# Four weight buffers at 32, 64, 128 and 256 bytes past multiples of 2048: a float32 network in three-product form

## The reference

```
h = rms_norm(x, norm_mlp[i])                                  # (512, 1024)
x = x + jnp.square(jax.nn.relu(h @ w_mlp_up[i])) @ w_mlp_down[i]
x = x + (p[i] @ w_ple_proj[i]) * jax.nn.sigmoid(x @ w_ple_gate[i])
...
u = h @ w_in                                                  # third block
ff = jnp.square(jax.nn.relu(h2 @ w_ff1)) @ w_ff2
```

## Time and profile before

| | us |
|---|---|
| runs of the kernel | 3722.1, 3724.81, 3724.98 (median 3724.81) |
| the profiled execution, its own time | 3728.49 |
| its span, first to last instruction | 3726.7 |
| TensorE busy (PE) | 3385.8 (91%) |
| TensorE weight loads (PEld), beside PE | 2664.8 (72%) |
| VectorE busy | 2026.8 (54%) |
| ScalarE busy | 1304.6 (35%) |
| GpSimd busy | 393.0 (11%) |
| DMA, mean rate over the span | 74 GB/s |

### The profile page before, as it was taken

The page is one execution under the profiler, slowest core; times in us unless marked ns, Lnnn a source line. Parts: engine busy times, 40 slices in busy tenths (PEclk is TensorE's granted clock), DMA queues, the critical chain, the costliest instruction groups (busy, mean ns, idle before and its releaser), DMA issues.

```text
span 3726.7 us, 50818 instructions
## 1 busy us (share of the span) xinstructions
PE 3385.8 (91%) x20970; PEld 2664.8 (72%) x20970; DVE 2026.8 (54%) x3555; ACT 1304.6 (35%) x2143; POOL 393.0 (11%) x336
## 2 busy tenths in 40 slices
PE   6898899999899999998996889978999989999998
PEld 4667777777676677786765666566777767777886
DVE  5454446664423456654555435578787872455443
ACT  3233233222323332223333234455555532324221
POOL 0001200000000000000001000035444520000000
PEclk9898899999898999999997989999999998999999
DMA  3120024442352124432320120031111102232321
GB/s 126 60 68 1 1 80 133 135 139 76 69 96 60 35 96 136 136 113 80 113 66 19 47 85 12 29 97 40 39 39 42 55 5 85 69 117 91 102 92 67
DMA packets 318853, 274.90 MB, mean 74 GB/s; under 512 B 10913, under 2 KB 310049, under 8 KB 317857
## 3 DMA queue, kind: packets, MB, share of 16 engines
q1 hardware_dynamic: 314368, 256.07, 22.7%
q10 hardware_dynamic: 4256, 15.58, 1.1%
HBM read 265.34 MB, written 6.29 MB: 73 GB/s over the span
## 4 chain that ended last, share of the span: by engine, by line
PE 77%; DVE 13%; ACT 5%; issue 3%; DMA 1%; POOL 1%; DVEq 0%; ACTq 0%; SPq 0%; POOLq 0%
PE ps L95 75%; DVE f L107 4%; DVE f L101 3%; DVE r L101 3%; PE ps L98 2%; ACT f L88 2%; DVE f L104 1%; ACT r L92 1%; ACT L88 1%; POOL f L101 1%; ACT f L92 1%; DVE f L113 1%; DVE f L110 1%; ACT f L89 0%; DVE r L107 0%
## 5 line engine op out<-in xcount | busy, mean ns | idle before, releaser
L95 PE MATMUL ps<-r,r 128*128 128x512 f32 x10368 | 2463.7, 396 | 124.0 <-DVE r L101 88.1
L95 PEld LDWEIGHTS ps<-r,r 128*128 128x128 f32 x10368 | 1928.5, 190 | 604.1 <-issue 183.1
L95 PE MATMUL ps<-f,f 64*64 64x64 f32 (+10 forms) x9648 | 878.0, 274 | 169.4 <-issue 48.6
L95 PEld LDWEIGHTS ps<-f,f 64*64 64x64 f32 (+4 forms) x9648 | 654.1, 161 | 366.6 <-issue 181.1
L101 DVE TENSOR_TENSOR r<-f,r 128x1024 fp32r<-128x1024 f32 (+2 forms) x621 | 657.8, 1065 | 464.2 <-ACT r L92 457.3
L92 ACT ACTIVATE r<-f 128x1024 fp32r<-128x1024 f32 (+2 forms) x548 | 506.6, 937 | 782.9 <-PE ps L95 661.7
L92 ACT ACTIVATE f<-ps 128x512 f32<-128x512 f32 (+3 forms) x422 | 189.8, 465 | 639.9 <-PE ps L95 388.2
L101 POOL TENSOR_TENSOR f<-f,f 128x512 f32<-128x512 f32 (+2 forms) x280 | 350.9, 1267 | 489.0 <-ACT f L88 273.6
L107 DVE SCALAR_TENSOR_TENSOR f<-f,f,f 128x128 f32<-128x128 f32 (+3 forms) x622 | 365.2, 592 | 26.5 <-ACT f L88 7.3
L101 DVE TENSOR_TENSOR f<-ps,f 128x512 f32<-128x512 f32 (+4 forms) x325 | 178.0, 560 | 340.3 <-PE ps L95 330.2
L88 ACT ACTIVATE f<-ps 128x512 f32<-128x512 f32 (+3 forms) x203 | 112.0, 553 | 622.3 <-PE ps L95 620.2
(11 more groups left out here) (32 smaller groups left out, 741.3 us busy)
## 6 DMA issues: line engine op xcount, KB each, us to landing
f<-in_w_mlp_up SPq DMA_DIRECT2D x32, 1024.0 KB, 6.0
f<-in_w_mlp_down SPq DMA_DIRECT2D x32, 1024.0 KB, 6.2
f<-in_w_ff SPq DMA_DIRECT2D x32, 1024.0 KB, 5.1
f<-in_w_ada SPq DMA_DIRECT2D x48, 512.0 KB, 3.9
f<-in_w_in SPq DMA_DIRECT2D x24, 1024.0 KB, 4.9
f<-in_w_in SPq DMA_DIRECT2D x44, 512.0 KB, 3.5
f<-in_w_in_even SPq DMA_DIRECT2D x12, 1024.0 KB, 5.2
f<-in_w_in_odd SPq DMA_DIRECT2D x12, 1024.0 KB, 12.4
```

Of the source, the lines that this page charges most:

```text
L95: return self.e.matmul(out, l, r, start=first, stop=last)
```

## The change

The allocation of the two high and the two low weight buffers. Before each, `K.at` is moved on, so that the buffers start at these distances past a multiple of 2048 bytes: the high ones 8 and 16 words (32 and 64 bytes), the low ones 32 and 64 words (128 and 256 bytes).

```
-        self.whi = [K.take(1024)[1] for _ in range(2)]
-        self.wlo = [K.take(1024)[1] for _ in range(2)]
+        self.whi, self.wlo = [], []
+        for home, phase in ((self.whi, 8), (self.whi, 16), (self.wlo, 32), (self.wlo, 64)):
+            K.at += (phase - K.at - K.slab // 4) % LINE if phase < LINE else (phase - K.at - K.slab // 4) % 128
+            home.append(K.take(1024)[1])
```

## The result

The changed kernel takes 3758.99 us (median of 4 runs, 3752.86 to 3768.01) against 3724.89 us before: a ratio of 1.0092, 95% interval 1.0075 to 1.0108, or +28 to +40 us. The forecast was 3757 us.

A forecast was written before the change was run, and what follows sets the result against it. The prediction took TensorE's rate of one-pass products as the bound; 7,500 products at 4.3 ns gave +32 us, all other terms 0, so 3724.8 + 32 = 3757 us, 0.9% slower. The range was 3720 to 3815 us, holding 0.79.

The forecast's parts named there:

- What bounds the kernel: TensorE, busy 91% of the span: the time is the rate of its one-pass products, 226.7 ns from start to start.
- The price of a product: One-pass products with shifted stationary operands: 231.0 ns instead of 226.7, so 4.3 ns more for each.
- the piece with 8 columns: Existing weight piece whose tiles start 32 bytes apart; its products took 231.0 ns, from which the 4.3 ns price was read.
- The count: One-pass products that pay the price: 7,500 taken, at least 5,957, at most all 9,984; +32 us in all.
- The grid: Weight buffers leaving multiples of 512 bytes cost 4.3 ns a product; 256 bytes was given the same price as 128.
- Moving operands: Weights streamed from shifted buffers: 5 us at most, counted 0; some 2,000 products streaming later stages' activations already in the count.
- ScalarE and VectorE: The 416 copies and 416 subtractions at the new addresses: taken as 0.
- Plain float32: Products at 431 ns a record, 2.2 ns beyond the columns each pass; used to bound a possible gain at -104 us.
- TensorE's busy time: In the profile after the change, PE busy time up by some 30 us.
- no change: Rival, 3725 us: the 4 ns come from the narrow load or 32-byte steps, not the buffer's start; chance 0.26.
- Faster: Rival, 3622 to 3690 us: the 13.3 ns are a stream-load collision at equal addresses modulo 512, resolved by shifting; chance 0.19.
- Much slower: Rival, 3800 to 3825 us: each product loses a further 13.3 ns, a rate of 240 ns; chance 0.13.

The follow-up runs named there:

- high alone: Against the kernel before: high buffers at 32 and 64 bytes, low ones at 0, region behind the buffers at 256 bytes; 3766.75 us, ratio 1.0098.
- narrow_pitch: Against the kernel before: narrow weight pieces (8 and 24 columns) stored 256 bytes from one kt to the next, not 32 and 96; 3724.57 us, ratio 0.9997.

## Why the prediction was right, and where its steps were not

- **What bounds the kernel:** right. The loss of 35.3 us is in the one-pass products, and TensorE's unbroken pieces got longer in proportion (2.0% in the yardstick), with nothing else moved.
- **The price of a product:** forecast 231.0 ns, 4.3 more; measured 231.4 in the window above, 4.7 more. One of the two places that it was read from, the piece with 8 columns, did show the cause (the narrow pieces at 256 bytes apart). That the products behind a wait have the same 231 is not shown to be the same thing. That the size fits to 0.4 ns is in part luck: the piece is a mix of seven distances, the change another mix, and single distances cost from 2.2 to 6.7 ns.
- **The count:** right. Compared product by product in the two traces (those whose next product starts within 260 ns in both), 7,570 products that had 226 or 227 ns before have 231.6 on the mean after, and 1,550 others went from 231.7 to 232.1, as the prediction had it for those behind waits. The forecast took 7,500.
- **The grid:** wrong. I took a start off the multiples of 512 bytes for the cause, and gave 256 bytes the price of 128. The low buffer at 256 bytes is free, and so is all at 256. The total came out since the piece that uses it also uses a high buffer at 64 bytes, and a piece with some costly loads pays most of the price: high alone costs the whole loss. This is luck.
- **What is measured from where:** not seen. I looked at the address of the load alone. In this change x, h and hh stay at multiples of 2048 bytes and the region at one of 256, so the address of the load and its distance from the stream are the same number, and the forecast could be right with the wrong one. With x shifted and the weights in place the loss is +0.83%, with both shifted alike it is none that can be told.
- **Moving operands:** counted at 0, with "some 2,000" for those of the stages. They are 2,880 of the 9,984 (2,976 with those of 256 columns), and at 256 bytes they are free. The 432 products of 512 columns in which the weights stream were put at nothing too; with buffers at 32, 64 or 128 bytes they have a price like the others, some 2 us.
- **ScalarE and VectorE:** 0, as forecast.
- **Plain float32:** its 431 ns were misread. The products overlap at the change of kind; by length they are (7.03 - 0.59) / 15 = 429 ns apart, 0.59 us being the duration of one in the groups by form of that stretch, so 1.3 ns a pass lie beyond the columns and not 2.2. The bound of the faster rival moves by some 9 us, the forecast not at all.
- **TensorE's busy time:** forecast +30 us, measured +45.1, of which 9.6 are the clock of this execution.
- **The rivals:** no change fell with the result itself, and its reasons, the narrow load or the steps of 32 bytes, were settled by the narrow pieces: the width has no part, the addresses have. Faster, with a collision at equal addresses that a shift resolves, is the reverse of what was found: equal addresses are the best of the seven distances measured (0, 32, 64, 128, 192, 224, where x is ahead of the weights, and 256 bytes). Distances that are no multiple of 32 bytes were not tried. Much slower was priced at 240 ns; the worst steady rate measured is 233.4.

That a weight load takes nothing from the running matmul, as the Trainium skill says ("TensorE: Matmul & The Clock Gate", Step-by-step), does not hold here to the last 3%: the same loads and streams run at 226.7 or at 233.4 ns a product by their distance alone. The Trainium skill (same page, Back-to-back issue gap) gives N/2.4 + 2.5 ns, 215.8 for 512 columns, as the gap of an isolated matmul. No steady stretch of one-pass products of any kernel here, all with a load beside each, reached it.

## What to carry to other kernels

Where a weight load runs beside a stream of a one-pass float32r product, let both start at the same place modulo 256 bytes; it needs neither multiples of 2048 nor of 256, and padding one side alone is what costs. Look at the distance from start to start in an unbroken stretch, to 0.1 ns: in these kernels a steady 226.7 with a duration of 389 ns is the good state, a pattern that averages 229 to 233 with 391 to 396 ns is another, and a price of 2 to 3% of TensorE's time shows in no wait and on no other engine. When one address moves by padding, all that is taken behind it moves too, so read the whole list of what starts where.

## What was not expected of the hardware

- The price depends on the distance between two reads modulo 256 bytes and is not symmetric: 6.7 ns a product at 32 and 64 bytes, 5.7 at 128, 2.2 at 192 in the last stage but 6.7 in another stretch of the same kernel, and 6.7 again at 224 (x at 32 bytes, weights at 0). Since all streams beside one another start at the same place modulo 256, the runs do not show whether it is the stream of the product itself or the one during which the load runs.
- Prices do not add up. With high buffers at 32 bytes and low ones at 128, or 64 and 256, the rate was 231.4 ns, better than with all of them at 32 or all at 128. It was better too than the 232.6 ns of the high ones alone, though the low ones are then at 0, which is free by itself, while 128 is not. So the distances tell whether there is a price, not always how much.
- The good rate is a state that products settle into, within some ten after a wait; 8-column loads at distance 0 kept it where they came upon it; in narrow_pitch, in the one piece that began behind a wait, they did not reach it.
- What the 13.3 ns beyond the 512 columns are that even the good state has stays open. No address tried took any of them away.
